# Attention heads of two layers: all 32 in pairs, a free piece behind each new pair, scores and outputs of a pair alternating between halves of the TensorE array

## The reference, cut to what matters

```python
for l in range(DEPTH_2):                       # 2 layers
    h = rmsnorm_2(x, norm_mix[l])
    proj = jnp.einsum('bsd,de->bse', h, w_in[l])
    qa, ka, va, qb, kb, vb, qc, kc, vc = jnp.split(proj, IN_SPLITS, axis=-1)
    oa = window_attention(...)                 # heads A0..A7: bias, window, sink
    ob = neighborhood_attention(...)           # heads B0..B7: bias and column mask
    oc = axial_global_attention(...)           # heads C0..C15: normed and rotated q, k
    mix = jnp.concatenate([rmsnorm_2(oa, ...), rmsnorm_2(ob, ...), rmsnorm_2(oc, ...)], axis=-1)
    x = x + jnp.einsum('bse,ed->bsd', mix, w_o[l])
    h = rmsnorm_2(x, norm_mlp[l])
    u = jax.nn.relu(jnp.einsum('bsd,df->bsf', h, w_up[l]))
    x = x + jnp.einsum('bsf,fd->bsd', u * u, w_down[l])
```

## Time and profile before

| what | value |
|---|---|
| median of 3 runs | 3492.25 us (3490.22 to 3498.49) |
| profiled execution, device time | 3494.03 us |
| its span, first to last instruction | 3492.4 us |
| mean granted TensorE clock | 0.97 |
| TensorE busy | 3306.4 us (95%) |
| VectorE busy | 2265.7 us (65%) |
| ScalarE busy | 1429.8 us (41%) |
| chain that ended last | PE 83%, DVE 9%, DMA 4%, issue 2%, ACT 2% |

### The profile page before, as it was taken

One profiled execution on the slowest core, in us unless ns is written; L12 is line 12 of the kernel. 1 busy time (PEld: TensorE's weight loads), 2 busy tenths in 40 slices (PEclk: granted clock), 3 DMA queues, 4 the chain that ended last, 5 costly groups with the idle time before them and its releaser, 6 DMA issues.

```text
span 3492.4 us, 63817 instructions
## 1 busy us (share of the span) xinstructions
PE 3306.4 (95%) x27350; PEld 3203.3 (92%) x27350; DVE 2265.7 (65%) x2517; ACT 1429.8 (41%) x1418; POOL 158.2 (5%) x292
## 2 busy tenths in 40 slices
PE   5999978999999998989999999999998999999998
PEld 5998878999999997878999999998877999999998
DVE  5888868565665675567655555557566855555555
ACT  3343333344444443444533333334344543333333
POOL 2111101000000000011000000000001000000000
PEclk6899988999999999999999999999999999999999
DMA  9888868655555543334555555555433455555553
GB/s 377 293 294 319 295 229 295 201 193 192 192 193 192 193 161 118 118 121 143 188 194 194 193 194 194 193 182 158 132 104 127 154 188 193 193 193 194 193 194 134
DMA packets 320750, 681.70 MB, mean 195 GB/s; under 512 B 14768, under 2 KB 21620, under 8 KB 320164
## 3 DMA queue, kind: packets, MB, share of 16 engines
q1 hardware_dynamic: 286272, 562.74, 48.4%
q0 software_dynamic: 31232, 109.07, 8.5%
q10 hardware_dynamic: 3108, 7.89, 0.6%
HBM read 677.47 MB, written 7.94 MB: 196 GB/s over the span
## 4 chain that ended last, share of the span: by engine, by line
PE 83%; DVE 9%; DMA 4%; issue 2%; ACT 2%; POOL 0%; ACTq 0%; DVEq 0%; POOLq 0%; SPq 0%
PE G L655 49%; PE Dn L655 33%; DVE w_lo L1162 2%; PE Dn L658 1%; DVE ada_acc L1282 1%; DMA ada_raw<-in_w_ada 1%; DMA raw<-in_w_in 1%; ACT w_hi L2022 1%; DMA zT<-in_w_ada 1%; DMA raw<-in_w_out 1%; DVE sq L1206 0%; DVE negmax L1558 0%; DVE xT L1820 0%; DVE s_sb L1555 0%; DVE s_sb L1551 0%
## 5 line engine op out<-in xcount | busy, mean ns | idle before, releaser
L655 PE MATMUL G<-h_hi,w_hi 128*128 128x256 f32 x5760 | 1626.4, 282 | 26.1 <-DVE w_lo L1162 13.6
L2022 ACT CAST w_hi<-raw 128x2048 fp32r<-128x2048 f32 (+2 forms) x536 | 1016.9, 1899 | 1470.5 <-DMA raw<-in_w_down 430.0
L655 PE MATMUL G<-h_lo,w_hi 128*128 128x256 f32 x5760 | 1612.2, 280 | 0.0
L655 PE MATMUL G<-h_hi,w_lo 128*128 128x256 f32 x5760 | 1611.5, 280 | 0.0
L1162 DVE TENSOR_TENSOR w_lo<-raw,w_hi 128x2048 fp32r<-128x2048 f32 (+2 forms) x536 | 1219.1, 2274 | 571.2 <-ACT w_hi L2022 569.8
L655 PEld LDWEIGHTS G<-h_hi,w_hi 128*128 128x128 f32 x5760 | 1100.5, 191 | 39.9 <-issue 21.6
L655 PEld LDWEIGHTS G<-h_lo,w_hi 128*128 128x128 f32 x5760 | 1099.8, 191 | 0.4
L655 PEld LDWEIGHTS G<-h_hi,w_lo 128*128 128x128 f32 x5760 | 1099.0, 191 | 0.0
L655 PE MATMUL Dn<-act_hi,w_hi 128*128 128x256 f32 x2752 | 762.2, 277 | 7.4 <-DVE act_lo L1674 7.4
L655 PE MATMUL Dn<-act_lo,w_hi 128*128 128x256 f32 x2752 | 761.7, 277 | 0.0
L655 PE MATMUL Dn<-act_hi,w_lo 128*128 128x256 f32 x2752 | 761.6, 277 | 0.0
(11 more groups left out here) (239 smaller groups left out, 1650.3 us busy)
## 6 DMA issues: line engine op xcount, KB each, us to landing
raw<-in_w_up SPq DMA_DIRECT2D x128, 1024.0 KB, 5.3
raw<-in_w_down SPq DMA_DIRECT2D x128, 1024.0 KB, 5.0
raw<-in_w_in SPq DMA_DIRECT2D x88, 1024.0 KB, 5.2
ada_raw<-in_w_ada POOLq DMA_DIRECT2D x152, 512.0 KB, 6.4
raw<-in_w_ffn_gate SPq DMA_DIRECT2D x44, 1024.0 KB, 5.0
raw<-in_w_ffn_up SPq DMA_DIRECT2D x44, 1024.0 KB, 5.0
raw<-in_w_ffn_down SPq DMA_DIRECT2D x44, 1024.0 KB, 5.0
raw<-in_w_o SPq DMA_DIRECT2D x32, 1024.0 KB, 5.1
```

Of the source, the lines that this page charges most:

```text
L655: return nc.tensor.matmul(o, lhsT, rhs, start=start, stop=stop, skip_group_check=True)
L2022: s.copy(w_hi[j][:, 0:PIECE_K * n], raw[j][:, 0:PIECE_K * n]).then_inc(hi_done, 1)
```

## The change

It changes the table of starts. Twelve heads of each layer started alone, one behind another; now C12 and C13, C14 and C15, B4 and B5, B6 and B7, A0 and A1, A2 and A3 start in one slot, and the slot behind starts none. Slots with a pair before keep it. The order of the heads is the same, and so are the eight heads of the first block.

It also changes the order within a slot. With a new pair, both heads' transposes of `done` come first, then the waits of both new heads, and then the four score products alternate between the two heads; each head's last product still signals its own scores. With a finished pair, TensorE waits for both heads' copied probabilities and then alternates the four output products.

```diff
-    starts = {13: "C12", 14: "C13", 15: "C14", 16: "C15", 21: "C4 C5", 22: "C6 C7", 23: "C8 C9", 24: "C10 C11",
-              25: "C0 C1", 26: "C2 C3", 28: "B4", 29: "B5", 30: "B6", 31: "B7", 32: "B0 B1", 33: "B2 B3",
-              34: "A0", 35: "A1", 36: "A2", 37: "A3", 38: "A4 A5", 39: "A6 A7"}
+    starts = {13: "C12 C13", 15: "C14 C15", 21: "C4 C5", 22: "C6 C7", 23: "C8 C9", 24: "C10 C11",
+              25: "C0 C1", 26: "C2 C3", 28: "B4 B5", 30: "B6 B7", 32: "B0 B1", 33: "B2 B3",
+              34: "A0 A1", 36: "A2 A3", 38: "A4 A5", 39: "A6 A7"}
...
+            def out_mm(H, kind, h, k):
...
+                return mm(o, v[:, k, :], pT[H % 2][:, k, :], k == 0, k == QT - 1)
...
+            def score(H, kind, h, t):
                 r0 = 64 * (h % 2)
                 qt_, kt_ = qk_tiles(kind, h)
+                return mm(SC[H % 2][:, t, :], zT[r0:r0 + 64, qt_, t * P:(t + 1) * P], zT[r0:r0 + 64, kt_, :],
+                          t == 0, t == 1)
+
+            def score_pair(new, base):
+                for H, kind, h in new:
+                    score_waits(kind, h, base + H)
                 for t in range(QT):
-                    i = mm(SC[H % 2][:, t, :], zT[r0:r0 + 64, qt_, t * P:(t + 1) * P], zT[r0:r0 + 64, kt_, :],
-                           t == 0, t == 1)
-                i.then_inc(qk_done, 1)
+                    for H, kind, h in new:
+                        i = score(H, kind, h, t)
+                        if t == QT - 1:
+                            i.then_inc(qk_done, 1)
 
             def slot(done, new, base):
 
+                pair = len(new) == 2
                 for n in range(max(len(done), len(new))):
                     if n < len(done):
                         H, kind, h = done[n]
                         finish(H, kind, h, base + H, 0)
-                    if n < len(new):
+                    if n < len(new) and not pair:
                         H, kind, h = new[n]
                         scores(H, kind, h, base + H)
-                if done:
+                if pair:
+                    score_pair(new, base)
+                if len(done) == 2:
                     misc_open(out_name(done), mbase[0])
                     for H, kind, h in done:
-                        i = finish(H, kind, h, base + H, 1)
+                        out_waits(kind, h, base + H)
+                    for k in range(QT):
+                        for H, kind, h in done:
+                            i = out_mm(H, kind, h, k)
                     i.then_inc(misc_w, 1)
+                elif done:
+                    misc_open(out_name(done), mbase[0])
+                    H, kind, h = done[0]
+                    finish(H, kind, h, base + H, 1).then_inc(misc_w, 1)
```

More of the change, by code:

```diff
@@ L812, in finish, with out_waits @@
                     return
+                out_waits(kind, h, no)
+                for k in range(QT):
+                    i = out_mm(H, kind, h, k)
+                return i
+            def out_waits(kind, h, no):
                 pe.wait_ge(pt_copied, no + 1)
@@ L815, in finish @@
                     pe.wait_ge(v_turned, h + 1)
+                else:
+                    pe.wait_ge(v_turned, lay[0] * len(V2_TILES) + (HEADS1 + v_need(kind, h)[1]))
+            def out_mm(H, kind, h, k):
+                if kind == "F":
                     o, v = MISC, v_tok[:, :, h * P:(h + 1) * P]
                 else:
-                    c, need = v_need(kind, h)
-                    pe.wait_ge(v_turned, lay[0] * len(V2_TILES) + (HEADS1 + need))
+                    c = v_need(kind, h)[0]
                     o = MISC[64 * (h % 2):64 * (h % 2) + 64, :]
                     v = v_tok[:, :, c:c + 64]
-                for k in range(QT):
-                    i = mm(o, v[:, k, :], pT[H % 2][:, k, :], k == 0, k == QT - 1)
-                return i
+                return mm(o, v[:, k, :], pT[H % 2][:, k, :], k == 0, k == QT - 1)
             def scores(H, kind, h, no):
@@ L836, in scores, with score_waits @@
                     return
+                score_waits(kind, h, no)
+                for t in range(QT):
+                    i = score(H, kind, h, t)
+                i.then_inc(qk_done, 1)
+            def score_waits(kind, h, no):
                 pe.wait_ge(exp_done, no - 1)
```

## The result

The changed kernel is slower: 3527.55 us (median of 4 runs, 3526.03 to 3528.83) against 3493.08 us for the kernel before in the same session, a ratio of 1.0089 with a 95% interval of 1.0074 to 1.0104. The forecast was 3500, its range ended at 3511. The profiled execution has a span of 3525.2 us, 32.8 more than before.

The account below looks back on a forecast made before the run. TensorE's work plus the waits between its instructions bounds the kernel. Two layers of +2.0 us from the slots and +2.0 from the clock give +8 on 3492.25, so 3500; own range 3495 to 3503, with rivals 3485 to 3511.

Parts of the forecast that it names:

- the clock's term: Longer idle at slots 14, 16, 29, 30, 34 and 37 lets TensorE's clock fall to half: 2.0 us a layer, bounds 0 and 5.
- my sum without the clock: Gains and losses of all slots, place by place, without further clock falls: +2.0 us a layer, two layers.
- Rival 3: Clock stays at half from slot 29 to 34, four further falls a layer: +14 us, 3506, slower by over 0.3%; 30%.
- C slots: Slots of the C heads, C12 to C15 and C0 to C11 together: -2.1 and -1.15 us a layer.
- slot 28 to piece 32: Heads B4 to B7 started as pairs: TensorE waits longer on VectorE's chains and the swap's copy, +4.65 us a layer.
- slots 32 to 34: Slot 33's scores both end later, so VectorE starts 1.36 us later and a wait grows: +0.85 us a layer.
- behind slot 34: The A heads, slots 34 to 40: gains and waits on VectorE nearly cancel, -0.2 us a layer, from -3 to +2.
- C0 to C11: Five pair-to-pair slots, each 0.23 us shorter in the new order: -1.15 us a layer.
- C12 to C15: Slots 14 to 17, these heads now started as pairs: the rotation at 1397.36 starts at 1395.3, -2.1 us a layer.
- Rival 1: TensorE's side decides and VectorE's chains fit into the free pieces: -6 us a layer, 3480; 7%.
- Rival 2: Gain and loss cancel, no further clock fall, slot 30's wait hidden: about -1 to +1 us a layer, 3492; 18%.
- Rival 4: Alternation itself halves a pair's outputs, 0.73 us in 16 slots, -11.7 us: with the rest 3488; 3%.

Follow-up runs that it names:

- e9: The changed kernel with a finished pair's outputs in the old order, both products of the first head and then both of the second: 3506.76 us, ratio 1.0028.
- e10: The changed kernel with a new pair's scores in the old place and order, each head's behind its own transposes, outputs still alternating: 3520.50 us, ratio 1.0064.
- e3: The changed kernel with unread matmuls of 128 columns filling TensorE's waits in the mixers: 3490.83 us, ratio 0.9977 to the kernel before.
- e7: The kernel before (old table, old order) with unread matmuls of 128 columns in TensorE's waits in the mixers: 3485.25 us, ratio 0.9956.
- e14: e3 with its extra matmuls cut from 128 to 2 columns, same number, places and waits: 3531.80 us, ratio 1.0100 to the kernel before.

## Why the prediction was wrong

**The step that failed is the clock's term.** I took 2.0 us a layer, from one and a half further falls at 1.3 us each, bounds 0 and 5. The half-speed time of the mixers grew from 31.7 to 105.2 us. At the slope of 0.38 that is 28 us, 14 a layer, nearly three times my upper bound; what is left of the 31.6 us is 3.8, and my sum without the clock was +4. The price was right: the fall that I priced, 1.3 us, is at half speed for 3.4 us (1540.6 to 1544.0), which is 0.38 too. The amount was wrong. The extra half speed is that of 11 such falls a layer and not of one and a half. In the trace the stretches that begin in the mixers went from 7 to 18, and four of them, behind the slots 16 and 29, last 10.2 us. Rival 3 had the mechanism ("the clock decides"), and its point of decision, three further falls a layer, was passed; it was mis-sized in the same way, with four falls at 1.3 us each.

Two steps behind that term were wrong.

- *Which waits count.* I read from the trace that waits of 2.16 us and more had a fall behind them and that 1.44 us and less did not, and looked for long waits one by one. That holds in layer 1 of the kernel before and not in its layer 2. There the clock falls at 2544.1, behind waits of 0.48, 0.52, 1.12 and 0.46 us, and at 2469.0, with one wait of 0.46 us before it and sixteen sums of two columns (a row of the timeline, then the window of the fall):

```profile
2466.32 1.95 PE L655 MATMUL Dn<-halves,sq 128*128 128x2 f32 x16 [0.46 <-ACT zT L2200]
...
2469.00:2472.40 3.40, 3.40 (x18) 3.40 (x17) 3.09 (x14) 0.00 (x0) 0.00 (x0) 0.50 0.00 0
```

  The same sums in layer 1 have no fall behind them. So in the trace before, short waits close together stood before one fall, and work of few columns before another. Slot 16 of the changed kernel fell with no wait over 1.43 us. I had its waits in the working (0.77, "another 0.46 to 0.55", the wait for the second copy) at the price of each and never added them up over the stretch. The Trainium skill (TensorE: Matmul & The Clock Gate, "A second HAM failure mode: psum-queue depth-cycling") says that frequent short idle times between groups of matmuls make the clock swing between its levels; slot 16, at a mean clock of 0.67 over 15.68 us, agrees. What exactly sets off a fall these runs don't settle.
- *A slot that ends at the same time was taken for equal.* "Alternated, both halves wait for that copy and then take 1.02, and the end is the same." It came 0.2 us later in each such slot. More than that, the outputs in block order kept the array at work while the copy ran, and e9 shows that the outputs' order is worth some 21 us. It is the same with the scores between the two transposes: I knew that they covered the copy's 0.77 and booked their move as a gain of 0.23 a slot; put back, they are worth 9 us (e10).

**The rest of the sum held, if the clock is taken out.** The filled pair shows it. e3 less e7 in the mixers is +3.0 us, against a sum of 2 x 2.0 = +4; by the ratios it is +7, with an uncertainty of as much. By parts, cut at slot 28's first scores, piece 32's first matmul and the piece behind slot 34, layer 1 and layer 2:

| part | forecast | e3 less e7 |
|---|---|---|
| C slots | -2.1 - 1.15 = -3.25 | -1.9 (with 3.4 us more at half speed in e3) and -3.3 (with the same) |
| slot 28 to piece 32 | +4.65 | +3.2 and +3.4 |
| slots 32 to 34 | +0.85 | +1.0 and +1.0 |
| behind slot 34 | -0.2 | -0.35 and -0.2 |

From slot 28 on neither kernel has any half speed. The two are not filled alike, so a part's difference can be the fill's.

In the changed kernel itself: slot 24 at 4.00 us (4.02), idle 4.58 at slot 29 (4.4), 5.56 behind the swap (5 to 6), slots 28 to 31 +5.7 (+4.65), C0 to C11 -0.8 (-1.15). C12 to C15 came to +3.9 in place of -2.1, the pieces from slot 17 to 21, where nothing was moved, to +1.0, and slots 32 to 34 to +4.2 in place of +0.85: in all three the clock fell. Slot 35 to the end of the heads came to +0.3 (-0.2).

Rival 1 (TensorE's side decides) fell with the measured waits. Rival 2 (no further fall) needed a clock that this kernel has only when it is filled (e3). Rival 4 fell: eight output records take 1.08 us alternated and 1.09 in block order.

## What to carry to other kernels

A reordering that ends at nearly the same time is not free if it turns work into idle time: where matmuls cover a copy, moving them away costs little in the sum of durations and can let the clock fall. Before trusting such a sum, add up the waits and the small operations of each slot with its neighbours, and compare with places of the same trace where the clock fell and where it held; price a fall by the time at half speed (here 0.38 us per us) and not as one piece each. Look at every layer before taking a rule from one. Where a stretch can't be kept at work otherwise, unread matmuls of 128 columns in the waits held the clock here, and were worth 0.44% on the kernel before and 1.1% on the changed one.

## What the runs showed of the hardware that I had not expected

- Forty records of a float32 matmul of 2 columns take 4.69 us (e14, mean clock of the stretch 0.88) and forty of 128 columns 4.63 (e3, 1.00), each with its weights loaded ahead (0.12 us a record). The width doesn't set the rate there, and yet the clock falls with the one and holds with the other.
- Recorded busy time doesn't tell the clock: e14 is busy for 92.5% (274.16 of 296.30) of a layer's mixer at a mean clock of 0.92, e7 for 93.5% (262.17 of 280.50) at 0.99.
- Two edits of +7 to +8 us each made +31 together, as their times at half speed did (+27.0 and +27.6 alone, +73.5 together). Where the clock carries the loss, effects of edits need not add.
